# A two-layer decoder trunk: first unit by feature chunk, fused last norm, fp32 router logits, selection by counting, and a first expert turn of its own

## The chip, the cores and the metric

The kernel runs on one core of a Trainium2 chip (trn2). Its time is that of the device, in microseconds, as the median of several runs. TensorE (PE) multiplies, VectorE (DVE), ScalarE (ACT) and GpSimd (POOL) do the elementwise work, and SyncE (SP) issues most transfers. Each engine works through its own queue in order and waits on semaphores.

## The reference

256 tokens of 1024 features pass through two layers, all in float32. Only the parts that the change touches are shown.

```python
for i in range(DEPTH):                                     # DEPTH = 2
    h = rmsnorm(x, g_mix[i])
    u_pool, v_conv, gate_logits = split(h @ w_in[i])       # pooling, conv, gates
    x = x + (gate_pool * y_pool + gate_conv * y_conv) @ w_mix_out[i]
    h = rmsnorm(x, g_xattn[i]); m = rmsnorm(mem, g_mem[i])
    x = x + memory_cross_attention(h, m, w_xq[i], w_xkv[i], w_xo[i])
    h = rmsnorm(x, g_ffn[i])
    if i % 2 == 0: x = x + swiglu(h, w_ffn_gu, w_ffn_down)
    else:          x = x + moe_swiglu(h, w_router, b_router, w_moe_gu, w_moe_down)
return rmsnorm(x, g_final)
# moe_swiglu: logits = h @ w_router + b_router; the two largest of 8 are taken (the lower
# index wins a tie), gates = softmax over the two; each token is the gated sum of its experts
```

## The kernel before

Every large product is computed from two halves of each operand: a high part, rounded to the fast float32 format of TensorE, and the rest. `mm3` issues three products for one: high by high, high by low, low by high. ScalarE makes the high part by a copy (`hi(n)` for weights into `WH`, `norm_hi` for features into `XH`), VectorE the low part by a subtraction (`lo(n)` into `WL`, `norm_lo` into `XL`).

The weights come in units of 128 x 2048 values, 1 MB, in a fixed order (`stream_plan` for the NA units of the two layers, `expert_units` for the 33 of one expert). SP loads them into a ring of 4 slots, and of 11 during the experts; the split halves have 3 slots. Before it loads a slot again SP waits until VectorE has split what was in it. In the program of each engine the order is written out by hand: at unit n, ScalarE and VectorE first split unit n + 2 and then do what belongs to unit n. The banks of PSUM are given out by a plan (`BankPlan`), and `claim` waits for whoever reads a bank's contents of before.

At the start SP issues the two token tiles of x (`xs`), unit 0, the small vectors as rows, and then the other units. ScalarE squares x in four pieces, VectorE makes the variance (L1144), GpSimd the factor (`rstd`, a power, L724), VectorE scales both tiles (L1151), TensorE transposes them into features (16 transposes, L1586) and then the vector rows, VectorE copies the vectors out (L1198 to L1200), and the chunks of features are split (L869 and L1160). Unit 0 multiplies by output tile: all eight chunks for the first 128 columns, then for the second. After unit 1 TensorE transposes the normalised memory (`norm_T("mem", 0)`), which ScalarE has loaded through its own queue and squared, and VectorE has scaled.

After the last unit of layer 1 comes the router. x is transposed, weighted with the gain and split as for any norm; the logits are made feature-major with `mm3` (L1830), copied out and transposed back to tokens (L1841). VectorE scales them, adds the bias, and picks the two largest by maxima and priorities (L1399 to L1413). TensorE ranks the chosen tokens with a triangular product (L1845 to L1850), VectorE builds the one-hot matrix `PMr` from the slots, and TensorE gathers the first expert's rows from the split, normalised x (`gather`, L1861, 32 products of 256 columns). GpSimd computes each token's places in the expert blocks and sends the rows there with indirect transfers. Then the turns: seven to fifteen in a loop (seven here), and a last one written out, each one expert block of 128 rows by 33 units of twelve products. Rows of experts after the first are loaded and transposed during the turn before. In the last turn the results of the earlier turns are added to x in eight pieces (`add_early`, at steps 16 to 23).

At the end VectorE adds the last expert's part, ScalarE squares x in four pieces, VectorE multiplies by the final gain in four pieces (L1546), the factor is made, ScalarE scales tile 0 and VectorE tile 1 (L1123 and L1551), and four stores go out.

## Time and profile before

| | us |
|---|---|
| Median of 3 runs (lowest to highest) | 1464.66 (1464.15 to 1464.69) |
| The profiled execution | 1463.53 |
| Its span, from first to last instruction | 1461.7 |
| TensorE busy in the span | 1420.4 |
| VectorE busy | 1145.3 |
| ScalarE busy | 909.8 |
| Mean granted TensorE clock, share of full | 0.99 |

The profile's times are read from the start of the span. A matmul counts as busy until its modelled end, so back-to-back products overlap, and busy time is no count of work. A row of busy time by window gives the window, its length, then for PE, PEld (TensorE's weight loads), DVE, ACT and POOL the busy us and the number of instructions, then TensorE's granted clock as a share of full (1.00 is 2.4 GHz, 0.50 is 1.2 GHz), the mean busy share of the DMA engines and GB/s. The bracket behind a row of a timeline is the idle time of the engine before it, with the one that ended it.

### The profile page before, as it was taken

The page shows a single profiled execution, that of the slowest core. Times are in us where ns is not written, and L with a number is a line of the kernel's source. Part 1 is how long each engine was busy: PE and PEld are TensorE (multiplying, and loading weights), DVE is VectorE, ACT ScalarE, POOL GpSimd, SP SyncE. Part 2 cuts the span into 40 slices and gives each one's busy share as a digit, 9 for nine tenths or more (in the row PEclk, how much of TensorE's full clock was granted, in tenths as well). Part 3 has the DMA queues.
Part 4 walks back from the last instruction along what each step waited for, and adds up shares of the span by engine and source line. Part 5 has one row for each costly group of instructions (what it writes and reads, how often), then busy time and mean ns, then how long its engine had stood idle before and what let it go on. Part 6 is the DMA issues. An engine that isn't in the chain of part 4 may idle for free.

```text
span 1461.7 us, 20187 instructions
## 1 busy us (share of the span) xinstructions
PE 1420.4 (97%) x7551; PEld 1226.0 (84%) x7551; DVE 1145.3 (78%) x1045; ACT 909.8 (62%) x825; POOL 72.2 (5%) x108
## 2 busy tenths in 40 slices
PE   6999999999999998998999999999999999999997
PEld 6998898888879997886888888888888888888875
DVE  6897855564547997745888888888889889898997
ACT  6444455544344435554677777777777777777774
POOL 1005000000000004000400000000000000000100
PEclk9999999999999999999999999999999999999998
DMA  9565953555554554547899999999999999999990
GB/s 293 171 190 173 340 207 116 185 189 194 181 198 148 190 171 145 173 141 305 306 394 354 400 397 368 392 369 390 395 362 393 378 381 395 361 395 387 379 369 29
DMA packets 189207, 413.13 MB, mean 283 GB/s; under 512 B 8830, under 2 KB 94174, under 8 KB 189150
## 3 DMA queue, kind: packets, MB, share of 16 engines
q1 hardware_dynamic: 184078, 397.62, 75.1%
q0 software_dynamic: 3328, 12.58, 2.3%
q10 hardware_dynamic: 1744, 2.13, 0.4%
q8 instruction: 40, 0.66, 0.2%
q14 instruction: 17, 0.14, 0.0%
HBM read 397.10 MB, written 15.20 MB: 282 GB/s over the span
## 4 chain that ended last, share of the span: by engine, by line
PE 82%; issue 10%; DVE 3%; ACT 2%; POOL 2%; DMA 1%; POOLq 0%; ACTq 0%; SPq 0%; DVEq 0%
PE bank L1569 26%; PE bank L1571 26%; PE bank L1570 26%; PE bank L1897 1%; DVE WL L1138 1%; DVE arena L1183 1%; ACT WH L850 1%; PE bank L1799 0%; PE bank L1818 0%; DMA xrows<-ysb 0%; POOL xn L740 0%; PE bank L1904 0%; PE bank L1602 0%; PE bank L1586 0%; PE bank L1861 0%
## 5 line engine op out<-in xcount | busy, mean ns | idle before, releaser
L1460 DVE TENSOR_TENSOR WL<-arena,WH 128x2048 fp32r<-128x2048 f32 x262 | 596.9, 2291 | 81.2 <-ACT WH L1064 81.2
L1064 ACT ACTIVATE WH<-arena 128x2048 fp32r<-128x2048 f32 x262 | 502.7, 1919 | 127.6 <-PE bank L1571 127.5
L1569 PE MATMUL bank<-WH,XH 128*128 128x512 f32 x1008 | 397.0, 394 | 0.5 <-issue 0.3
L1571 PE MATMUL bank<-WH,XL 128*128 128x512 f32 x1008 | 393.1, 390 | 0.0
L1570 PE MATMUL bank<-WL,XH 128*128 128x512 f32 x1008 | 392.6, 389 | 0.0
L1138 DVE TENSOR_TENSOR WL<-arena,WH 128x2048 fp32r<-128x2048 f32 x109 | 248.5, 2283 | 108.7 <-ACT WH L850 108.7
L850 ACT ACTIVATE WH<-arena 128x2048 fp32r<-128x2048 f32 x109 | 205.9, 1894 | 61.0 <-PE bank L1571 58.9
L1571 PEld LDWEIGHTS bank<-WH,XL 128*128 128x128 f32 x1008 | 189.2, 188 | 39.9
L1569 PEld LDWEIGHTS bank<-WH,XH 128*128 128x128 f32 x1008 | 189.4, 188 | 39.4 <-issue 1.1
L1570 PEld LDWEIGHTS bank<-WL,XH 128*128 128x128 f32 x1008 | 189.5, 188 | 38.0
L1569 PE MATMUL bank<-XH,WH 128*128 128x256 f32 x592 | 169.4, 286 | 5.1 <-DVE XL L1160 3.4
L1570 PE MATMUL bank<-XL,WH 128*128 128x256 f32 x592 | 168.4, 284 | 0.0
L1571 PE MATMUL bank<-XH,WL 128*128 128x256 f32 x592 | 168.3, 284 | 0.0
L1569 PE MATMUL bank<-WH,hThm 128*128 128x512 f32 x352 | 138.9, 395 | 0.4 <-DVE WL L1460 0.4
L1571 PE MATMUL bank<-WH,hTlm 128*128 128x512 f32 x352 | 137.3, 390 | 0.0
L1570 PE MATMUL bank<-WL,hThm 128*128 128x512 f32 x352 | 137.1, 390 | 0.0
L1569 PEld LDWEIGHTS bank<-XH,WH 128*128 128x128 f32 x592 | 114.3, 193 | 6.5 <-issue 3.7
L1570 PEld LDWEIGHTS bank<-XL,WH 128*128 128x128 f32 x592 | 114.5, 193 | 0.1
L1571 PEld LDWEIGHTS bank<-XH,WL 128*128 128x128 f32 x592 | 114.4, 193 | 0.0
L1183 DVE SCALAR_TENSOR_TENSOR arena<-arena,vec 128x256 f32<-128x256 f32 x240 | 97.9, 476 | 0.0
L1569 PEld LDWEIGHTS bank<-WH,hThm 128*128 128x128 f32 x352 | 66.1, 188 | 14.6 <-DVE WL L1460 1.3
L1571 PEld LDWEIGHTS bank<-WH,hTlm 128*128 128x128 f32 x352 | 66.1, 188 | 14.0
(246 smaller groups left out, 1357.3 us busy)
## 6 DMA issues: line engine op xcount, KB each, us to landing
arena<-in_w_moe_gu SPq DMA_DIRECT2D x128, 1024.0 KB, 5.4
arena<-in_w_moe_down SPq DMA_DIRECT2D x88, 1024.0 KB, 7.2
arena<-in_w_moe_gu SPq DMA_DIRECT2D x96, 512.0 KB, 6.1
arena<-in_w_in SPq DMA_DIRECT2D x28, 1024.0 KB, 4.9
arena<-in_w_ffn_gu SPq DMA_DIRECT2D x44, 512.0 KB, 4.6
arena<-in_w_xkv SPq DMA_DIRECT2D x16, 1024.0 KB, 5.3
arena<-in_w_ffn_down SPq DMA_DIRECT2D x11, 1024.0 KB, 4.8
arena<-in_w_mix_out SPq DMA_DIRECT2D x8, 1024.0 KB, 5.0
```

Source lines behind the costliest of these rows:

```text
L850: a.activation(WH[:, n % HL, 0:width(n)], s[:, 0:width(n)], ACT.Copy).then_inc(hi_ready, 1)
L1064: a.activation(WH[:, (NA + i) % HL, :], raw[s], ACT.Copy).then_inc(hi_ready, 1)
L1138: v.tensor_tensor(WL[:, n % HL, 0:w], s[:, 0:w], WH[:, n % HL, 0:w].bitcast(F32), ALU.subtract).then_inc(lo_ready, 1)
L1183: v.scalar_tensor_tensor(acc[:, c, :], cu[:, c, k:k + S], tap(L, k, c), acc[:, c, :], ALU.mult, ALU.add).then_inc(conv_step, 1)
L1460: v.tensor_tensor(WL[:, (NA + i) % HL, :], raw[(i % NM) % RING_M], WH[:, (NA + i) % HL, :].bitcast(F32), ALU.subtract).then_inc(lo_ready, 1)
L1569: te.matmul(out, ah, bh, start=start, stop=False, skip_group_check=shared)
L1570: te.matmul(out, ah, bl, start=False, stop=False, skip_group_check=shared)
L1571: return te.matmul(out, al, bh, start=False, stop=stop, skip_group_check=shared)
L1897: ins = te.transpose(ps[:, c * P:c * P + P], hhm[:, o:o + P], ident[:, :])
```

## The change

It makes five edits.

- **Start.** g_mix is loaded ahead of unit 0, and unit 0 in two halves; unit 1 follows, then the other vectors; the memory's load moves to SP's queue, behind unit 2. VectorE squares tile 1 and scales tile 0, ScalarE squares tile 0 and scales tile 1. TensorE first multiplies an identity 11 and 7 times, transposes g_mix alone, and computes unit 0 by chunk: both output tiles for chunk 0, then for chunk 1, and so on. The other vectors are transposed after unit 0.
- **Logits.** The unscaled x is transposed, copied as fp32 into `xT`, and multiplied in fp32, tokens on the output partitions, by router weights that have taken the gain (`wrg`). Six unused products follow (`WARM`).
- **Selection.** Each logit is compared with each other one; the counts give its rank, the two top ranks are chosen.
- **Gather.** The first expert's rows are gathered in fp32 from x itself; the one-hot matrix carries the norm's factor and the copies out of PSUM the gain. The first turn is written out on TensorE: its gathers 0 to 2 come before unit 0, gather 3 behind it, and each unit waits for its own chunks. The other engines keep their loop.
- **Last norm and early adds.** Only one piece is multiplied by the gain apart; the other three are scaled and weighted in one VectorE instruction each, behind the variance. The early adds stand at steps 13, 14, 17, 18, 21, 22, 25 and 26.

```diff
 HL = 3
+WARM = 6
+EARLY_AT = (13, 14, 17, 18, 21, 22, 25, 26)
+WARM_UP = (11, 7)
...
-            sp.dma_start(wdst("a", 0), wsrc(*units[0])).then_inc(raw_landed[0], 16)
-            r = 0
-            for src in (g_mix, g_xattn, g_mem, g_ffn, pool_scale, b_dw, conv_ln_g, conv_ln_b):
+            sp.dma_start(rows[0:DEPTH * KC, 0, :], g_mix.rearrange("l (k p) -> (l k) p", p=P)).then_inc(gmix_in, 16)
+            sp.dma_start(wdst("a", 0)[:, 0:4], wsrc(*units[0])[:, 0:4]).then_inc(first_half, 16)
+            sp.dma_start(wdst("a", 0)[:, 4:8], wsrc(*units[0])[:, 4:8]).then_inc(raw_landed[0], 16)
+            sp.dma_start(wdst("b", 1), wsrc(*units[1])).then_inc(raw_landed[1], 16)
+            r = DEPTH * KC
+            for src in (g_xattn, g_mem, g_ffn, pool_scale, b_dw, conv_ln_g, conv_ln_b):
...
-            for n, (kind, L, j) in list(enumerate(units))[1:]:
+            for n, (kind, L, j) in list(enumerate(units))[2:]:
+                if n == 3:
+                    sp.dma_start(mem_in, mem[0].rearrange("(t p) d -> p t d", p=P)).then_inc(mem_in_s, 16)
...
-            squares(norm_id("mix", 0), xs, BY_TILE, lambda i, t: (x_in[t], 16))
-            hi(0)
-            act.dma_start(mem_in, mem[0].rearrange("(t p) d -> p t d", p=P)).then_inc(mem_in_s, 16)
+            act.wait_ge(c_one, 1)
+            a.activation(unused[:, 0:1], ones[:, 0:1], ACT.Square)
+            act.wait_ge(x_in[0], 16)
+            a.activation(xn[:, 0, :], xs[:, 0, :], ACT.Square, scale=D ** -0.5,
+                         accum_out=ss[:, 0, 0, 0:1]).then_inc(sq_done, 2)
+            act.wait_ge(first_half, 16)
+            a.activation(WH[:, 0, 0:1024], raw[0][:, 0:1024], ACT.Copy).then_inc(hi_half, 1)
+            act.wait_ge(rstd_ready, 1)
+            a.activation(xn[:, 1, :], xs[:, 1, :], ACT.Copy, scale=rs[:, 0, 1:2]).then_inc(x1_scaled, 1)
...
+            for b in range(4):
+                act.wait_ge(*full(("norm", 0, b)))
+                if b == 0:
+                    a.activation(XH[:, 0, :], bk(("norm", 0, 0))[:, 0:S], ACT.Copy,
+                                 scale=gcol("mix", 0, 0)).then_inc(first_hi, 1)
...
+                if b == 1:
+                    act.wait_ge(raw_landed[0], 16)
+                    a.activation(WH[:, 0, 1024:2048], raw[0][:, 1024:2048], ACT.Copy).then_inc(hi_ready, 1)
...
+                if (kind, L, j) == ("xo", 1, 2):
+                    x_squares("ffn", L, "xo", 0)
+                    for i in range(2):
+                        act.wait_ge(*full(("xT", i)))
+                        a.activation(xT[:, 2 * i:2 * i + 2, :], bk(("xT", i))[:, :].rearrange("p (c s) -> p c s", c=2),
+                                     ACT.Copy).then_inc(xT_early, 1)
...
+                    act.wait_ge(x_gained, 4)
+                    for t in range(NT):
+                        a.activation(xn[:, t, :], xn[:, t, :], ACT.Copy, scale=rs[:, N, t:t + 1]).then_inc(xn_ready, 1)
...
-                    a.activation(XH[:, 2 * b:2 * b + 2, 0:P], gathered(b), ACT.Copy).then_inc(g_hi, 1)
+                    for c in range(2):
+                        ins = a.activation(XH[:, 2 * b + c, 0:P], gathered(b)[:, c, :], ACT.Copy,
+                                           scale=gcol("ffn", 1, 2 * b + c))
+                    ins.then_inc(g_hi, 1)
...
-            norm_scale(norm_id("mix", 0), xs)
-            lo(0)
+            dve.wait_ge(x_in[1], 16)
+            v.scalar_tensor_tensor(xn[:, 1, :], xs[:, 1, :], 1.0 / D, xs[:, 1, :], ALU.mult, ALU.mult,
+                                   accum_out=ss[:, 0, 1, 0:1]).then_inc(sq_done, 2)
+            dve.wait_ge(sq_done, 4)
+            v.tensor_scalar(vv[:, 0, :], ss[:, 0, :, 0], EPS, None, ALU.add).then_inc(var_ready, 1)
...
+            v.tensor_scalar(xn[:, 0], xs[:, 0], rs[:, 0, 0:1], None, ALU.mult).then_inc(xn_ready, 2)
+            dve.wait_ge(hi_half, 1)
+            v.tensor_tensor(WL[:, 0, 0:1024], raw[0][:, 0:1024], WH[:, 0, 0:1024].bitcast(F32),
+                            ALU.subtract).then_inc(lo_half, 1)
...
+                if b == 1:
+                    dve.wait_ge(hi_ready, 1)
+                    v.tensor_tensor(WL[:, 0, 1024:2048], raw[0][:, 1024:2048], WH[:, 0, 1024:2048].bitcast(F32),
+                                    ALU.subtract).then_inc(lo_ready, 1)
...
+                def x_with_gain(m):
+                    for t in range(NT):
+                        dve.wait_ge(sq_done, 4 * norm_id("ffn", 1) + 2 * m + t + 1)
+                        ms = slice(m * 512, m * 512 + 512)
+                        v.tensor_tensor(xn[:, t, ms], xs[:, t, ms], gain_rows[:, ms], ALU.mult).then_inc(x_gained, 1)
...
+                    def xT_copy(i, t, c0, nc_):
+                        dve.wait_ge(*full(("xT", i)))
+                        v.tensor_copy(xT[:, c0:c0 + nc_, t * P:t * P + P],
+                                      bk(("xT", i))[:, 0:nc_ * P].rearrange("p (c s) -> p c s", c=nc_)
+                                      ).then_inc(xT_late, 1)
+                    xT_copy(2, 0, 4, 4)
+                    xT_copy(3, 1, 4, 2)
+                    norm_var(norm_id("ffn", L))
+                    xT_copy(4, 1, 6, 2)
+                    x_with_gain(1)
...
+            link(v.tensor_tensor(beats[:, :, :, :], LOG.unsqueeze(3).to_broadcast([P, NT, NE, NE]),
+                                 LOG.unsqueeze(2).to_broadcast([P, NT, NE, NE]), ALU.is_ge))
+            link(v.tensor_tensor(beats[:, :, :, :], beats[:, :, :, :],
+                                 tri[:, :, :].unsqueeze(1).to_broadcast([P, NT, NE, NE]), ALU.mult))
+            v.tensor_reduce(BEATEN, beats[:, :, :, :].rearrange("p t a b -> p t b a"), X_AXIS, ALU.add
+                            ).then_inc(route, 1)
+            rt[0] += 1
+            link(v.tensor_reduce(BEATS, beats[:, :, :, :], X_AXIS, ALU.add))
+            link(v.tensor_tensor(RANK, BEATEN, BEATS, ALU.subtract))
+            ranks = top[:, :].unsqueeze(1).to_broadcast([P, NT, NE])
+            v.tensor_tensor(SEL, RANK, ranks, ALU.is_lt).then_inc(sel_ready, 1)
...
+                v.tensor_scalar(PM[:, t, :], iota[:, :], slotT[:, t, 0:1], rs[:, norm_id("ffn", 1), t:t + 1],
+                                ALU.is_equal, ALU.mult).then_inc(PM0_ready, 1)
...
+            gather_lo((0, 1), lambda b: b + 1)
+            lo(NA + 1)
+            gather_lo((2, 3), lambda b: b + 1)
...
-                    if last and 16 <= i < 24:
-                        add_early(i - 16)
+                    if last and i in EARLY_AT:
+                        add_early(EARLY_AT.index(i))
...
+            v.tensor_tensor(xv, xv, fin_gain[:, 0:4, :], ALU.mult).then_inc(gained, 1)
+            norm_var(N)
+            dve.wait_ge(rstd_ready, N + 1)
+            for r in range(1, 4):
...
+                v.scalar_tensor_tensor(xn[:, t, ms].rearrange("p (c s) -> p c s", c=4),
+                                       xs[:, t, ms].rearrange("p (c s) -> p c s", c=4), rs[:, N, t:t + 1],
+                                       fin_gain[:, 4 * m:4 * m + 4, :], ALU.mult, ALU.mult).then_inc(out_ready, 1)
...
+            for i in range(WARM_UP[0]):
+                te.matmul(bank[2][:, 0:P], ident[:, :], ident[:, :], start=True, stop=True)
+            pe.wait_ge(gmix_in, 16)
...
+            done(te.transpose(ps[:, 0:R0], rows[0:R0, 0, :], ident[0:R0, 0:R0]), ("vec",))
+            for i in range(WARM_UP[1]):
+                te.matmul(bank[2][:, 0:P], ident[:, :], ident[:, :], start=True, stop=True)
+            for kk in range(2):
...
+            to_feature_major("mix", 0, xn, lambda t: (x1_scaled, 1) if t else (xn_ready, 1), (1, 2, 3))
+            def other_vectors():
+                pe.wait_ge(gmix_in, 16)
+                pe.wait_ge(rows_in, 16 * (7 + 1 + 1))
+                ps = claim(("vec2",))
+                te.transpose(ps[:, 0:VROWS], rows[0:VROWS, 0, :], ident[0:VROWS, 0:VROWS])
+                R = TAPS * CC
+                for L in range(DEPTH):
+                    te.transpose(ps[:, P + L * R:P + L * R + R], rows[0:R, 1 + L, :], ident[0:R, 0:R])
+                done(te.matmul(ps[:, 504:504 + NE], ones[0:1, :], brow[0:1, :], start=True, stop=True), ("vec2",))
...
+                for k in range(KC):
+                    if k % 4 == 0:
+                        pe.wait_ge(*((lo_ready, 1) if k else (lo_half, 1)))
+                    pe.wait_ge(ht_lo if k else first_lo, k // 2 + 1)
+                    for ct in range(2):
+                        cs = slice(ct * P, ct * P + P)
+                        ins = mm3(ps[:, ct * S:ct * S + S], wh[:, k, cs], wl[:, k, cs], XH[:, k, :], XL[:, k, :],
+                                  (k, ct) == (0, 0), (k, ct) == (KC - 1, 1), True)
...
+                for kk in chunks:
+                    ins = te.matmul(bk(("logits",))[:, t * NE:t * NE + NE], xT[:, kk, t * P:t * P + P], wrg[:, kk, :],
+                                    start=(t, kk) == (0, 0), stop=(t, kk) == (1, KC - 1), skip_group_check=True)
...
+            pe.wait_ge(x_add, xadd(1, "xo", 2))
+            late_xT(2, 0, range(4, KC))
+            pe.wait_ge(wrg_ready, 1)
+            pe.wait_ge(xT_early, 2)
+            claim(("logits",))
+            logits(0, (0, 1))
+            pe.wait_ge(x_add, xadd(1, "xo", 3))
+            late_xT(3, 1, (4, 5))
+            late_xT(4, 1, (6, 7))
+            logits(0, (2, 3))
+            logits(1, range(4))
+            pe.wait_ge(xT_late, 1)
+            logits(0, range(4, KC))
+            pe.wait_ge(xT_late, 2)
+            logits(1, (4, 5))
+            pe.wait_ge(xT_late, 3)
+            done(logits(1, (6, 7)), ("logits",))
+            for i in range(WARM):
+                te.matmul(bank[4][:, :], XH[:, 0, 0:P], XH[:, 0:2, :].rearrange("p c s -> p (c s)"), start=True,
+                          stop=True)
+            pe.wait_ge(sel_ready, 3)
...
+                ps = claim(("gather", b))
+                for t in range(NT):
+                    pe.wait_ge(PM0_ready, t + 1)
+                    for c in range(2):
+                        kk = 2 * b + c
+                        ins = te.matmul(ps[:, c * 2 * P:c * 2 * P + P], xs[:, t, kk * P:kk * P + P], PM[:, t, :],
+                                        start=(t, c) == (0, 0), stop=(t, c) == (NT - 1, 1), skip_group_check=True)
+                done(ins, ("gather", b))
+            for b in range(3):
+                gather(b)
...
-                    if i == 0:
+                    if first and i == 1:
+                        gather(3)
+                    if first and i < 4:
+                        pe.wait_ge(g_lo, i + 1)
+                    if first and i == 4:
+                        for bb in (0, 5, 2, 3):
+                            pe.wait_ge(*read(plan.last[bb]))
...
-            with pe.Fori(0, n) as it:
+            turn_tensor(0, False, True)
+            with pe.Fori(1, n) as it:
                 turn_tensor(it, False)
```

## Rows read from the trace of the kernel before

**Rows 1.** The page of the profile, its first line and part 1

```profile
span 1461.7 us, 20187 instructions
...
PE 1420.4 (97%) x7551; PEld 1226.0 (84%) x7551; DVE 1145.3 (78%) x1045; ACT 909.8 (62%) x825; POOL 72.2 (5%) x108
```

**Rows 2.** Busy time by window, expert turns (columns: see the profile section)

```profile
795.00:888.00 93.00, 93.00 (x426) 77.21 (x425) 82.54 (x48) 70.87 (x51) 0.00 (x0) 1.00 1.02 389
...
sum 744.00, PE 743.22 PEld 615.52 DVE 662.23 ACT 564.04 POOL 19.15; mean PE 92.90 PEld 76.94 DVE 82.78 ACT 70.51 POOL 2.39
```

**Rows 3.** Who TensorE waited for: us in total, times, longest

```profile
PE bank L1586 <- DVE xn L1151: 9.1, 1, 9.1
...
PE bank L1845 <- DVE lg L1413: 3.6, 1, 3.6
...
PE bank L1569 <- DVE WL L1460: 0.6, 2, 0.4
```

**Rows 4.** Timeline of the first 20 us: start, us, engine, line, operation

```profile
4.47 0.63 ACT L857 ACTIVATE xn<-xs 128x512 f32<-128x512 f32 x1 [2.38 <-DMA xs<-in_x]
...
8.19 1.42 DVE L1151 TENSOR_SCALAR xn<-xs,rs 128x1024 f32<-128x1024 f32 x2 [0.92 <-POOL rs L724]
8.75 1.91 ACT L850 ACTIVATE WH<-arena 128x2048 fp32r<-128x2048 f32 x1 [1.66 <-DMA arena<-in_w_in]
...
9.09 4.03 PE L1586 MATMUL bank<-ident,xn 128*128 128x128 f32 x16 [9.09 <-DVE xn L1151]
...
15.27 2.65 ACT L869 ACTIVATE XH<-bank,vec 128x256 fp32r<-128x256 f32 x7
15.89 3.23 DVE L1160 SCALAR_TENSOR_TENSOR XL<-bank,vec,XH 128x256 fp32r<-128x256 f32 x8 [1.03 <-ACT XH L869]
...
16.91 0.36 PE L1569 MATMUL bank<-XH,WH 128*128 128x256 f32 x1 [2.75 <-DVE XL L1160]
```

**Rows 5.** Timeline of TensorE, the memory's transposes

```profile
29.98 1.91 PE L1586 MATMUL bank<-ident,xn 128*128 128x128 f32 x16
```

**Rows 6.** Busy time by window at the start

```profile
0.00:20.00 20.00, 8.03 (x37) 7.39 (x38) 8.56 (x17) 10.65 (x20) 4.17 (x21) 0.93 0.95 310
18.00:19.00 1.00, 1.00 (x6) 1.00 (x6) 1.00 (x3) 1.00 (x1) 0.00 (x0) 0.50 1.10 345
```

**Rows 7.** Timeline from the last sum of x to the rank product

```profile
682.26 0.69 DVE L1192 TENSOR_TENSOR xs<-xs,bank 128x512 f32<-128x512 f32 x1 [2.03 <-PE bank L1571]
...
689.30 0.35 DVE L1387 SCALAR_TENSOR_TENSOR lg<-bank,rs,bias 128x8 f32<-128x8 f32 x2
...
692.16 0.59 PE L1845 MATMUL bank<-lg,upper 128*128 128x8 f32 x2 [3.56 <-DVE lg L1413]
...
693.03 0.57 PE L1847 MATMUL bank<-lg,upper 128*128 128x8 f32 x2
```

**Rows 8.** Busy time by window around the router

```profile
690.00:692.00 2.00, 0.00 (x0) 0.00 (x0) 1.76 (x12) 2.00 (x2) 0.00 (x0) 0.50 0.80 317
...
698.00:700.00 2.00, 2.00 (x11) 2.00 (x11) 1.97 (x2) 0.52 (x2) 1.89 (x2) 0.50 0.00 0
```

**Rows 9.** Timeline of the first expert units

```profile
702.14 0.49 PE L1569 MATMUL bank<-WH,XH 128*128 128x512 f32 x1 [0.26 <-issue]
...
703.19 3.91 ACT L1064 ACTIVATE WH<-arena 128x2048 fp32r<-128x2048 f32 x2
...
705.14 4.49 DVE L1460 TENSOR_TENSOR WL<-arena,WH 128x2048 fp32r<-128x2048 f32 x2 [1.91 <-ACT WH L1064]
```

**Rows 10.** Timeline of the last norm and the stores

```profile
1454.13 0.19 ACT L857 ACTIVATION_READ_ACCUMULATOR xn<-xs 128x1 f32 x1
1455.28 0.15 DVE L1144 SCALAR_TENSOR_TENSOR vv<-ss 128x2 f32<-128x2 f32 x1
...
1455.51 1.11 POOL L724 TENSOR_TENSOR rs<-vv,mhalf 128x2 f32<-128x2 f32 x1 [78.91 <-DVE vv L1144]
...
1458.58 0.35 ACTq L1126 DMA_DIRECT2D out<-xn  x1
```

322 lines of the change are left out of this document (155 added, 167 removed).

## The prediction

> **What bounds the kernel now.** I read the page first, then who waited for whom on TensorE, then the busy time by stage, and last the timeline of the three stretches where TensorE stands still. The page shows a program that is TensorE's nearly everywhere: busy 97% of 1461.7 us [rows 1]. An expert turn of 93 us has it busy for all 93.00 us at full clock, with VectorE at 82.5 and ScalarE at 70.9, and over all eight turns it is busy 743.2 of 744 us [rows 2]. The diff leaves the arithmetic of a turn alone, so the turns can't become shorter. What is left is TensorE's idle time, and the waits say where it is [rows 3]: 9.1 us before the first transpose, 3.6 us in front of the router's rank product, and only 0.6 us inside the expert turns. The change works on three places: the start, the router up to the third expert unit, and the last norm. I cost each by the time at which TensorE (or the last store) leaves that place, since all that comes behind moves along with it.
>
> **Start, before.** x is squared from 4.47, both tiles are scaled by 9.6, 16 transposes take 4.03 us, then the gain vectors, then eight feature chunks on ScalarE (2.65 us for seven, 0.38 each) and VectorE (3.23 us for eight, 0.40 each); the first product issues at 16.91 [rows 4]. The first two units end where the memory transposes begin, 29.98 [rows 5]. The granted clock around 18 was 0.50, the lower level of 1.2 GHz, after 2.75 us without work [rows 4, 6]. Those 96 products in 13.1 us come out at 0.12 each at full clock, if the lower one lasted some 3.5 us.
>
> **Start, after, step by step.** Between 4.47 (tile 0 there) and 8.75 (unit 0 there) tile 1 and the two halves of unit 0 land, 1.43 us per half megabyte: tile 1 at 5.9, the first half at 7.3 [rows 4]. VectorE squares tile 1 in about 1.2 us (half of its 2.3 us subtraction, taken from the pair of 4.49 [rows 9]): 7.1. The way from variance to factor took 1.1 us before (7.1 to 8.19): 8.2, no gain yet. VectorE scales tile 0 (0.71) to 8.9. ScalarE splits half a unit (half of 1.91) from 7.3 and scales tile 1 in 1.0: 9.3. The first chunk's transposes run at once, its high half is copied by 10.1, its low half stands at 10.6; the pitch is 0.40 from there. The second half of unit 0's weights costs ScalarE 0.96 and VectorE 1.15 after chunk 3, so chunk 7 is complete at 15.3. Then unit 1: ScalarE (1.91) to 16.0, VectorE (2.3) to 18.3. TensorE does six products per chunk, 0.72 us at full clock, from 11.3 to 17.3, and the vector transposes that were moved behind them to 18.0. Unit 1 starts at 18.3, bound by its weights; 48 products of 0.12 are 5.75 us: end at 24.0. Saving against 29.98: **6.0 us**. If the whole first unit ran at 1.2 GHz it would end up to 1.5 us behind unit 1's weights: 4.5. The 18 warm-up products cost nothing, as TensorE has nothing else to do up to 9.3; without that cover each would cost 0.2 to 0.4.
>
> Moved along: the memory's load leaves ScalarE's queue and stands in SP's behind units 1 and 2 and the small vector loads. 310 GB/s over the first 20 us are 6.2 MB [rows 6]; x, three units, the vectors and the memory are 5.6, so it lands near 18.5. Squares (four pieces, 2.6 us), variance and power (1.1) and scaling (1.4) end near 23.6, and TensorE asks at 24.0. That cover is thin; behind it each us later costs one us, since unit 2 is queued behind these transposes.
>
> **Router, before.** The last sum of x ends at 682.95, logits start on VectorE at 689.30, TensorE gets the selection at 692.16 and does a small fp32 product in 0.43 us (two in 0.87) [rows 7]. The clock is 0.50 at 690 to 692 and still at 698 to 700 [rows 8]. The first expert product comes at 702.14; ScalarE starts on expert units 2 and 3 at 703.19 and VectorE at 705.14, so unit 2 is ready at 707.4 [rows 9]. Units 0 and 1 hold TensorE for 2 x 2.73 us (33 units of twelve products and some transposes fill a turn, at most 2.8 each [rows 2]), to 707.6: no stall.
>
> **Router, after.** x is transposed as it is, and 16 fp32 products with eight columns (32 instructions) replace the 24 split ones. No row has one at full clock. Bounds: 0.43 as read, and half of it, 0.22. With 0.22, eight transposes of 0.12 (1.91 for 16 [rows 5]) and 0.4 of wait for the late sum, logits are complete at 687.1. Selection on VectorE: two logit rows (0.35), then four operations over 128 elements, for which the nearest rows are 0.18 (eight elements [rows 7]) and 0.40 (256 elements [rows 4]); I take 0.29, then two short ones of 0.2: 1.9 us, selection at 689.0. Rank product and five short steps to 690.0, slots and first one-hot tile 690.4. The gather turns into fp32 with 128 columns, one product for two of 256: again 0.22 to 0.43. Three of four pieces, 12 products, take 2.7: 693.1. So expert unit 0 starts at 693.4, almost 9 us earlier. But that isn't kept. The fourth piece (0.9) now comes behind unit 0 (2.73): 697.1. ScalarE is a queue in order, and unit 2's split stands behind that copy: before, 1.3 us lay between the last gather product (702.14 less the issue gap of 0.26) and the split at 703.19; the copy in two parts adds 0.2. So the split runs from 698.6 to 700.5, VectorE to 702.8. TensorE is done with unit 1 at 699.9 and waits some 3 us; unit 2 starts at 702.9 to 703.5, against 707.6. I take **4.2 us**. Data isn't late: DMA stood still at 698 to 700 [rows 8], with the ring of eleven units full. The gained x (VectorE, four of 0.69) and its scaling (ScalarE, two of 1.0) end near 688, hidden: GpSimd wants them only after the slots. GpSimd's own steps, done by 702 before, feed a load of turn 0's later half.
>
> **Last norm.** The last read-out ends at 1454.32, but the variance starts at 1455.28, because three gain products stand ahead of it on VectorE; the power takes 1.11 us and the last store is issued at 1458.58 [rows 10]. After: variance at 1454.35, power between 0.72 (as at the start) and 1.11, then three fused products of 0.68 instead of two scalings of ScalarE in a row: the last store is ready at 1457.3 to 1457.7. Saving **1.0 us**. Spreading the early adds can recover at most the 0.6 us of waits inside the turns; I count nothing.
>
> **Sum.** 6.0 + 4.2 + 1.0 = 11.2 us. The profiled execution took 1463.53 us (its span and 1.8 around it) and would take 1452.3; the median of the runs is 1.1 above it, so I forecast 1453.5.
>
> **The clock, and what the skill says.** TensorE was at 1.2 GHz through both the router's small products and most of the gather, after 3.6 us without work [rows 7, 8]. The change fills part of that hole with useful products and six idle ones, and leaves less than 1 us in one piece. The Trainium skill, TensorE: Matmul & The Clock Gate (Part 1: The HAM clock gate), holds that the throttled state is the default, that only sustained activity lifts it, and that the switching point differs from run to run. If loads with eight columns aren't activity, the clock falls under the new router as under the old, which is rival (a); by that rule the saving would be 8.1 us or less, not 11.2. No row here settles it.
>
> **Rivals.** (a) *The router runs at 1.2 GHz.* For it: it did before. Against: the hole is shorter. Rank product and 12 gather products then cost 3.1 us more (0.2 each): 1456.6; with the logits slow too, 16 times 0.21, another 3 us: 1459.5. (b) *The start gives half.* Unit 0's first half or the memory lands 3 us late: 1456.5. For it: the DMA share is 0.95 over the first 20 us [rows 6], so nothing there has slack. Against: the byte count above. (c) *Slower than before.* TensorE's program now has the turn three times in its code. Were its instructions fetched too slowly, the pitch of the products in the turns would grow: 744 us of turns times 1.5% is 11.2 us, the point where it eats the gain; at 2.5% the time is 1472. Against: the loop of before fetches as many instructions in each turn and has no gap [rows 2].
>
> **Chances and range.** Forecast 0.52, (a) 0.28, (b) 0.14, (c) 0.03, and 0.03 for a hidden loss that cancels the gain. A measurement of this kernel can tell 0.2%, 2.9 us, from no change. So: faster 0.93 or a little more, within 0.04, slower 0.03. The range goes from the best prices (6.5, 4.8 and 1.2 us saved with a run at the low end, and the early adds' 0.6) to (a) nearly whole: 1451.3 to 1459.0.
>
> **What would show it.** The first product near 11 us and the memory transposes near 24; the selection at 689; the first expert product near 693, then a wait of TensorE of about 3 us for the weights of unit 2; the variance right behind the last square. I am wrong if the clock column has 0.5 from 688 on, if TensorE waits over 1 us for the memory rows, or if a turn takes more than 93.2 us.

## The result, and the profile after

The changed kernel takes 1456.36 us in the median of five runs (1453.81 to 1457.07), against 1464.15 (1461.93 to 1464.69, five runs) of the kernel before: ratio 0.9944, interval 0.9933 to 0.9955. By the medians that is 7.8 us less, by the ratio 8.2. I had forecast 1453.5. The profiled execution took 1454.71 us with a span of 1453.0, against a span of 1461.7 before [rows 1], so it gained 8.7 us.

The page's first line and part 1, and who TensorE waited for (us in total, times, longest):

```profile
span 1453.0 us, 20257 instructions
...
PE 1424.2 (98%) x7600; PEld 1230.7 (85%) x7600; DVE 1142.0 (79%) x1043; ACT 907.8 (62%) x817; POOL 70.8 (5%) x110
```

```profile
PE bank L1643 <- DVE WL L1535: 3.0, 1, 3.0
...
PE bank L1696 <- ACT xn L920: 1.2, 1, 1.2
...
PE bank L1660 <- DVE xn L1199: 1.1, 2, 0.8
```

The waits of 9.1 us ahead of the first transpose and of 3.6 ahead of the rank product [rows 3] are gone from the table. The first is only filled, though: the first transpose of x starts at 9.09 in both kernels, behind warm-up products now. New are 3.0 us for the weights of expert unit 2, 1.2 for tile 1 of x, and 1.1 for the memory rows.

**Start.** The timelines of ScalarE and TensorE, first 29 us:

```profile
8.46 1.06 ACT L918 ACTIVATE WH<-arena 128x1024 fp32r<-128x1024 f32 x1 [2.78 <-DMA arena<-in_w_in]
...
18.90 1.91 ACT L875 ACTIVATE WH<-arena 128x2048 fp32r<-128x2048 f32 x1 [2.10 <-DMA arena<-in_w_in]
21.74 0.63 ACT L882 ACTIVATE xn<-arena 128x512 f32<-128x512 f32 x1 [0.92 <-DMA arena<-in_mem]
```

```profile
10.99 1.47 PE L1660 MATMUL bank<-ident,xn 128*128 128x128 f32 x12
12.25 0.36 PE L1643 MATMUL bank<-XH,WH 128*128 128x256 f32 x1
...
26.20 0.30 PE L1660 MATMUL bank<-ident,xn 128*128 128x128 f32 x1 [0.79 <-DVE xn L1199]
26.77 1.86 PE L1660 MATMUL bank<-ident,xn 128*128 128x128 f32 x15 [0.27 <-DVE xn L1199]
28.39 0.36 PE L1643 MATMUL bank<-XH,WH 128*128 128x256 f32 x1
```

The first half of unit 0 is there at 8.46, where I had 7.3; the memory at 21.7, where I had 18.5. Unit 2's first product, behind the memory's transposes, comes at 28.39. Before, those transposes began at 29.98 [rows 5], and the product followed at 31.64: 3.3 us saved. The line of before, and DMA up to the memory's landing in the changed kernel:

```profile
31.64 0.36 PE L1569 MATMUL bank<-XH,WH 128*128 128x256 f32 x1
```

```profile
0.00:21.70 21.70, 18.04 (x125) 17.05 (x126) 11.76 (x18) 12.41 (x17) 4.55 (x23) 1.00 0.95 299
```

**Router.** VectorE's last sum of x and its split of unit 2, ScalarE's copies of gather pieces 2 and 3 and its splits, TensorE at unit 2:

```profile
678.90 0.69 DVE L1240 TENSOR_TENSOR xs<-xs,bank 128x512 f32<-128x512 f32 x1 [2.04 <-PE bank L1645]
...
697.63 4.49 DVE L1535 TENSOR_TENSOR WL<-arena,WH 128x2048 fp32r<-128x2048 f32 x2 [1.96 <-ACT WH L1113]
```

```profile
690.73 0.62 ACT L1095 ACTIVATE XH<-bank,vec 128x128 fp32r<-128x128 f32 x2 [0.27 <-PE bank L1996]
694.40 0.63 ACT L1095 ACTIVATE XH<-bank,vec 128x128 fp32r<-128x128 f32 x2 [3.05 <-PE bank L1996]
...
695.68 5.51 ACT L1113 ACTIVATE WH<-arena 128x2048 fp32r<-128x2048 f32 x3
```

```profile
700.07 0.76 PE L1643 MATMUL bank<-WH,XH 128*128 128x512 f32 x1 [2.97 <-DVE WL L1535]
```

ScalarE does nothing for 3.05 us between the third and the fourth copy, and its split of unit 2 stands behind both. Units 0 and 1 last only to 696.9. Busy time by window, with the granted clock in the third column from the right:

```profile
682.00:684.00 2.00, 2.00 (x13) 1.95 (x14) 0.40 (x3) 1.91 (x3) 0.00 (x0) 0.72 1.04 412
684.00:686.00 2.00, 2.00 (x6) 1.48 (x5) 1.80 (x9) 0.42 (x1) 0.00 (x0) 0.50 1.02 406
...
698.00:700.00 2.00, 0.00 (x0) 0.00 (x0) 2.00 (x2) 2.00 (x2) 1.75 (x1) 0.98 1.01 414
700.00:702.00 2.00, 1.93 (x5) 1.58 (x6) 2.00 (x1) 1.19 (x1) 1.92 (x2) 0.50 1.13 342
```

The clock is at 1.2 GHz twice. By windows of 1 us it falls at about 682.9, in the last of the logits (679.1 to 683.5), and stays down through the six idle products to 686.3; TensorE counts as busy all that time. It falls again at 699.9, as the wait for unit 2 ends. The long low stretch of before [rows 8] has become two.

The router ends, for this comparison, with TensorE's first hidden transposes of turn 0, in the kernel before and in the changed one:

```profile
726.78 1.04 PE L1897 MATMUL bank<-ident,sh 128*128 128x128 f32 x8
```

```profile
720.75 1.03 PE L2026 MATMUL bank<-ident,sh 128*128 128x128 f32 x8
```

Counted from the start of the last sum of x (682.26 [rows 7] and 678.90) that is 44.5 us before and 41.9 after: 2.7 us saved.

**Last turn and last norm.** The first three sets of hidden transposes of the last turn, and VectorE at the end:

```profile
1373.41 1.03 PE L2026 MATMUL bank<-ident,sh 128*128 128x128 f32 x8
...
1407.12 1.04 PE L2026 MATMUL bank<-ident,sh 128*128 128x128 f32 x8
...
1429.86 0.60 PE L2026 MATMUL bank<-ident,sh 128*128 128x128 f32 x4
```

```profile
1446.65 0.16 DVE L1192 SCALAR_TENSOR_TENSOR vv<-ss 128x2 f32<-128x2 f32 x1 [0.19 <-ACT xn L882]
1447.65 2.08 DVE L1623 SCALAR_TENSOR_TENSOR xn<-xs,rs,fin_gain 128x512 f32<-128x512 f32 x3 [0.84 <-POOL rs L749]
```

The transposes are 33.71 and 22.74 us apart. The kernel before had them at 1379.46, 1413.36 and 1437.57:

```profile
1413.36 1.04 PE L1897 MATMUL bank<-ident,sh 128*128 128x128 f32 x8
...
1437.57 0.60 PE L1897 MATMUL bank<-ident,sh 128*128 128x128 f32 x4
```

That is 33.90 and 24.21, so 1.66 us are gained inside the last turn. From the last square's sum to the end of the span it was 7.6 us (1454.13 [rows 10] to 1461.7) and is 6.6 (1446.43 to 1453.0): 1.0 us. The four parts, 3.3 + 2.7 + 1.7 + 1.0, are the 8.7 us of the spans in their tenths.

### The profile page after: what moved, and what is told of

It reads as the page before. It is cut to its first block, busy times and chain, and to the rows that moved or that the text cites. A ratio compares the mean times of both kernels' runs of the same rounds, so it can differ in the third digit from the quotient of the medians.

```text
span 1453.0 us, 20257 instructions
## 1 busy us (share of the span) xinstructions
PE 1424.2 (98%) x7600; PEld 1230.7 (85%) x7600; DVE 1142.0 (79%) x1043; ACT 907.8 (62%) x817; POOL 70.8 (5%) x110
## 4 chain that ended last, share of the span: by engine, by line
PE 86%; issue 6%; DVE 2%; ACT 2%; POOL 2%; DMA 1%; SPq 1%; ACTq 0%; POOLq 0%; DVEq 0%
PE bank L1643 27%; PE bank L1645 27%; PE bank L1644 27%; PE bank L2026 1%; PE bank L1920 1%; PE bank L1939 1%; DVE WL L1186 1%; DMA arena<-in_mem 1%; DVE arena L1231 1%; DMA xrows<-ysb 1%; POOL xn L765 0%; PE bank L2033 0%; ACT WH L875 0%; SPq L609 0%; PE bank L1676 0%
## 5 line engine op out<-in xcount | busy, mean ns | idle before, releaser
L1535 DVE TENSOR_TENSOR WL<-arena,WH 128x2048 fp32r<-128x2048 f32 x262 | 596.6, 2291 | 81.5 <-ACT WH L1113 81.4
L1113 ACT ACTIVATE WH<-arena 128x2048 fp32r<-128x2048 f32 x262 | 502.6, 1919 | 128.4 <-PE bank L1645 128.4
L1186 DVE TENSOR_TENSOR WL<-arena,WH 128x2048 fp32r<-128x2048 f32 (+1 forms) x108 | 246.3, 2284 | 108.0 <-ACT WH L875 108.0
L875 ACT ACTIVATE WH<-arena 128x2048 fp32r<-128x2048 f32 (+1 forms) x108 | 203.9, 1894 | 60.4 <-PE bank L1645 57.6
```

The costliest lines, as they stand in the source:

```text
L875: a.activation(WH[:, n % HL, 0:width(n)], s[:, 0:width(n)], ACT.Copy).then_inc(hi_ready, 1)
L1113: a.activation(WH[:, (NA + i) % HL, :], raw[s], ACT.Copy).then_inc(hi_ready, 1)
L1186: v.tensor_tensor(WL[:, n % HL, 0:w], s[:, 0:w], WH[:, n % HL, 0:w].bitcast(F32), ALU.subtract).then_inc(lo_ready, 1)
L1535: v.tensor_tensor(WL[:, (NA + i) % HL, :], raw[(i % NM) % RING_M], WH[:, (NA + i) % HL, :].bitcast(F32), ALU.subtract).then_inc(lo_ready, 1)
```

## The experiments

Each ratio is to the kernel before, run on the same chip. Times of that kernel there were 1463.5 to 1464.4 us in the median.

**e1: the early adds back where they were.**

```diff
-EARLY_AT = (13, 14, 17, 18, 21, 22, 25, 26)
+EARLY_AT = tuple(range(16, 24))
```

> The changed kernel with the eight early adds of the last turn back in steps 16 to 23, one per step. Theory (the adds overloaded VectorE): the last turn lost about 1.6 us in the kernel before, hidden in waits too short for the wait table, so this run is 1.6 us slower than the changed kernel, with the last turn's hidden transposes 33.9, 24.2 us apart again. Rival (the wait table is complete): at most 0.6 us slower, and the 1.65 us come from elsewhere, from the data or the DMA of that execution.

**e2: the kernel before, with the early adds spread.**

```diff
-                    if last and 16 <= i < 24:
-                        add_early(i - 16)
+                    if last and i in (13, 14, 17, 18, 21, 22, 25, 26):
+                        add_early((13, 14, 17, 18, 21, 22, 25, 26).index(i))
```

> The kernel before with only the places of the eight early adds changed to 13, 14, 17, 18, 21, 22, 25 and 26. Theory: 1.6 us faster than the kernel before (ratio 0.9989), all of it between the second and third set of hidden transposes of the last turn. Rival: 0.6 us or less, ratio 0.9996 or nearer to one.

e1 took 1458.46 us (0.9957, interval 0.9943 to 0.9971), 2.1 above the changed kernel. e2 took 1461.92 (0.9985, 0.9976 to 0.9994), 2.2 us under the kernel before. TensorE's timeline of e1, then of e2:

```profile
1409.61 1.04 PE L2026 MATMUL bank<-ident,sh 128*128 128x128 f32 x8
...
1433.93 0.60 PE L2026 MATMUL bank<-ident,sh 128*128 128x128 f32 x4
```

```profile
1414.20 1.04 PE L1897 MATMUL bank<-ident,sh 128*128 128x128 f32 x8
...
1436.94 0.60 PE L1897 MATMUL bank<-ident,sh 128*128 128x128 f32 x4
```

24.2 to 24.3 us with the adds in a row, 22.74 with them spread, in either kernel. The theory that the adds in a row cost some 1.6 us holds. VectorE's groups of the kernel before, 1402 to 1427 (busy us, mean ns, then idle before), show how:

```profile
L1460 DVE TENSOR_TENSOR WL<-arena,WH 128x2048 fp32r<-128x2048 f32 x9 | 20.6, 2284 | 0.0
L1490 DVE SCALAR_TENSOR_TENSOR xs<-early,early_gate,xs 128x512 f32<-128x512 f32 x4 | 3.0, 745 | 0.0
```

VectorE has no idle time there, and a split with an add (2.20 + 0.66) is issued every 2.87 us, while TensorE needs 2.73 for a unit. The waits are not all too short for the wait table, as my expectation had it: it lists two, of 0.2 and 0.4 us. But it counts only from a product's modelled end (0.39), which overhangs the next start (0.23) by 0.16. By the starts, the products at 1420.08 and 1429.27 come 0.36 and 0.56 us late, the one behind each takes 0.11 more, and one at 1410.51 comes 0.20 late and is not in the table. All starts more than 0.29 us apart, from the first hidden transposes of the last turn to the third, add up to 1.8 us beyond the 0.23 before and to 0.3 in the changed kernel.

**e3: all four gather pieces ahead of expert unit 0.**

```diff
-            for b in range(3):
+            for b in range(4):
                 gather(b)
...
-                    if first and i == 1:
-                        gather(3)
```

> The changed kernel with all four gather pieces in front of expert unit 0. Theory (ScalarE's queue: the split of unit 2 stands behind the copy of the fourth piece, and TensorE's clock falls only because of the 3.0 us wait): expert unit 0 starts about 0.9 us later, the copy of piece 3 ends about 2.7 us earlier, TensorE waits less than 0.5 us for unit 2, the granted clock stays at 1.00 from 686 on, and the kernel is 2.5 to 3.5 us faster than the changed one, near 1453. Rival 1 (the clock would fall anyway, as it follows the small router products): only the wait shrinks, 1.5 to 2 us. Rival 2 (VectorE's split of unit 2 is bound by VectorE's own queue): no gain, TensorE waits as before at unit 2.

1451.59 us (0.9912, 0.9899 to 0.9926), 4.8 under the changed kernel in the median, more than the 2.5 to 3.5 I had expected. Between the two profiles the router is 2.6 us shorter. ScalarE and TensorE:

```profile
694.49 0.63 ACT L1095 ACTIVATE XH<-bank,vec 128x128 fp32r<-128x128 f32 x2 [0.27 <-PE bank L1996]
...
695.79 3.72 ACT L1113 ACTIVATE WH<-arena 128x2048 fp32r<-128x2048 f32 x2
```

```profile
700.18 0.47 PE L1643 MATMUL bank<-WH,XH 128*128 128x512 f32 x1 [0.26 <-DVE WL L1535]
```

The wait is 0.26 us, and no low stretch follows it. Here the clock was low from 685.6 to 692.5, from the idle products through rank products and gather, so the part of the theory that the clock stays up from 686 on is wrong: the first low stretch is not caused by the wait, only the second is.

**e4: the memory's load on ScalarE's queue.**

```diff
-                if n == 3:
-                    sp.dma_start(mem_in, mem[0].rearrange("(t p) d -> p t d", p=P)).then_inc(mem_in_s, 16)
...
             a.activation(xn[:, 1, :], xs[:, 1, :], ACT.Copy, scale=rs[:, 0, 1:2]).then_inc(x1_scaled, 1)
+            act.dma_start(mem_in, mem[0].rearrange("(t p) d -> p t d", p=P)).then_inc(mem_in_s, 16)
```

> The changed kernel with the memory's load issued from ScalarE's queue, behind the scaling of tile 1 (about 10.5 us), and taken out of SP's queue in front of unit 3. Theory (the memory was late because it stood behind the others in SP's queue): it lands 1 to 3 us earlier than 21.7, ScalarE does its squares right behind the split of unit 2, the waits of 1.1 us at the memory's transposes go, and unit 1's end to the end of the memory transposes takes 2.0 instead of 3.2 us: 1 us faster than the changed kernel. Rival (DMA bandwidth is the limit: 310 GB/s): the memory lands earlier only as unit 2 or the vectors land later, so the gain is under 0.3 us or it is slower.

1459.28 us (0.9965, 0.9953 to 0.9977): 2.9 us above the changed kernel where I had expected 1 below. My theory fell. ScalarE and TensorE:

```profile
20.45 1.91 ACT L873 ACTIVATE WH<-arena 128x2048 fp32r<-128x2048 f32 x1 [3.64 <-DMA arena<-in_w_in]
```

```profile
27.01 0.30 PE L1659 MATMUL bank<-ident,xn 128*128 128x128 f32 x1 [1.60 <-DVE xn L1198]
27.58 3.45 PE L1659 MATMUL bank<-ident,xn 128*128 128x128 f32 x15 [0.27 <-DVE xn L1198]
```

The load was issued at 8.46 and no longer held up the squares, but unit 2 landed at 20.45 instead of 18.90, which fits the rival: one bandwidth is shared. The squares stand behind unit 2's split, so the wait at the memory's transposes grew from 0.79 to 1.60 us. The clock fell half a us behind it, stayed at 1.2 GHz for about 3.4 us, and fifteen transposes took 3.45 us for 1.86.

**e5: the kernel before, with the new start alone** (all edits of the start in the diff above, nothing else).

> The kernel before with the start of the changed one alone (first unit by chunks, warm-up products, the halves of unit 0, the memory's load in SP's queue); router, last norm and early adds as before. Theory (the traces show the start's whole gain and it is kept to the end): the memory transposes end 3.3 us earlier and the kernel is 3.3 us faster, ratio 0.9977. Rival 1 (my forecast for the start): 6.0 us, ratio 0.9959. Rival 2 (the gain is given back later): under 1 us.

1459.32 us (0.9972, 0.9961 to 0.9983): 4.1 us saved, interval 2.5 to 5.7. The 3.3 lies in it, the 6.0 does not, and nothing is given back. This execution alone saved 4.7 us (31.64 less 26.93, and as much in the span), so what the start is worth differs with the execution. In it unit 2 landed at 17.48, the memory's squares began at 20.28, TensorE did not wait, and unit 2's first product came at 26.93. In the profiles of the kernels that keep this start and its load order, that product came at 26.93 (e5), 27.08 (e7), 27.17 (e1), 27.87 (e8), 28.07 (e12), 28.29 (e3) and 28.39 (the changed kernel); in the three with the old start at 30.64 (e2), 31.64 and 31.79 (e11). The later ones are those in which unit 2 and the memory landed later.

**e6: e3, with the memory ahead of unit 2** on SP's queue, on ScalarE and on VectorE.

```diff
+            sp.dma_start(mem_in, mem[0].rearrange("(t p) d -> p t d", p=P)).then_inc(mem_in_s, 16)
             for n, (kind, L, j) in list(enumerate(units))[2:]:
-                if n == 3:
...
+                if (kind, L, j) == ("a", 0, 0):
+                    squares(norm_id("mem", 0), mem_in, BY_TILE, lambda i, t: (mem_in_s, 16))
                 if n < NA - 1 and (kind, j) != ("cout", 1):
                     hi(n + 2)
...
```

> The changed kernel with four gather pieces in front of expert unit 0 and, at the start, the memory's load put in front of unit 2's on SP's queue, its squares in front of the split of unit 2 on ScalarE, and its scaling in front of unit 2's low half on VectorE. Theory (all loads of the start share one bandwidth, so it is their order that counts): the memory lands near 19 and unit 2 near 21.7; the wait of 1.1 us at the memory's transposes goes and unit 2 is still in time (needed at 27.0): 1.0 to 1.3 us faster than with the four pieces alone, near 1450.5. Rival (unit 2 is now late, as it was with the memory on ScalarE's queue): TensorE waits after the memory's transposes instead, and the time is 1 to 3 us longer than 1451.6.

1450.83 us (0.9912, 0.9899 to 0.9926): by the times not to be told from e3. ScalarE's timeline shows the rest:

```profile
17.30 0.63 ACT L881 ACTIVATE xn<-arena 128x512 f32<-128x512 f32 x1 [0.62 <-DMA arena<-in_mem]
...
21.09 1.92 ACT L874 ACTIVATE WH<-arena 128x2048 fp32r<-128x2048 f32 x1 [1.22 <-DMA arena<-in_w_in]
```

TensorE has no wait at the memory's transposes any more, and unit 2's first product comes at 26.77, 27.02 and 26.87 in the three profiles with this order (e6, e9, e10). It takes the spread of 1.5 us out of the start, at its early end. In the profile of e6 the router gave the gain back: its low stretch lasted 10.2 us, against 6.8 in e3.

**e7: e3 without the six idle products (WARM = 0).**

> The changed kernel with four gather pieces in front of expert unit 0 and without the six idle products in front of the router's rank product. Theory (the clock falls because the products with eight columns and the wait for the selection keep TensorE too idle; it falls within the logits, ahead of the six products): the low stretch starts at most 1 us earlier and ends no later, and the time is within 1 us of 1451.6. Rival (the six products shorten the low stretch): the low stretch lasts 3 to 4 us longer, as with the kernel before (10 us), and the time is 1.5 us or more above 1451.6.

1452.58 us (0.9925, 0.9911 to 0.9938). The low stretch runs from 683.6 to 690.4, as long as in e3. The six products don't change it; TensorE waits 2.2 us for the selection in their place. The time is 1.0 us above e3, at the edge of the 1 us that the theory named. Its place for the fall was wrong in both: the logits end at about 684.4 in e3 and 682.7 in e7, and the clock falls at 685.6 during the idle products, and at 683.6 in the wait.

**e8: the changed kernel without the 18 warm-up products (WARM_UP = (0, 0)).**

> The changed kernel without the 18 warm-up products at the start. Theory (TensorE has idled in front of the first chunk, and the clock is then low through much of the first unit, as it was low at 17.4 to 20.8 in the kernel before): a stretch of 3.4 us or more at 1.2 GHz within 12 to 20 us; the first unit is bound by its products there, and the memory's transposes come 0 to 1.5 us later than 25.4, so the kernel is up to 1.5 us slower than the changed one. Rival (the start is bound by loads, not by TensorE): no difference, as the wait for the memory's rows takes it up.

1457.02 us (0.9955, 0.9942 to 0.9969), not to be told from the changed kernel. TensorE's transposes of x and its first product, and a window behind them:

```profile
10.84 2.68 PE L1660 MATMUL bank<-ident,xn 128*128 128x128 f32 x12
13.26 0.38 PE L1643 MATMUL bank<-XH,WH 128*128 128x256 f32 x1
```

```profile
12.00:16.00 4.00, 4.00 (x31) 4.00 (x30) 3.24 (x7) 4.00 (x8) 0.00 (x0) 1.00 1.11 301
```

No low stretch lies in the first unit, whose products follow each other every 0.12 us. So my theory fell in the place it named. But the warm-up does something: without it the twelve transposes take 2.68 us instead of 1.47, 421 ns each as in the kernel before instead of 272, though the clock column reads 1.00 there in all three. The first product comes 1.0 us later than in the changed kernel, although the first half of unit 0 landed 0.5 us earlier (8.00). The changed kernel's lead is lost at the memory, which lands at 21.7 there and at 21.2 here: unit 2's first product comes at 28.39 and at 27.87. The rival's end came true, and the two profiles fit its reason.

**e9: e6 with wider logits products**, and **e12: the changed kernel with them alone.** Only the first 8 of the 64 columns are read.

```diff
...
-                    ins = te.matmul(bk(("logits",))[:, t * NE:t * NE + NE], xT[:, kk, t * P:t * P + P], wrg[:, kk, :],
+                    ins = te.matmul(bk(("logits",))[:, t * 64:t * 64 + 64].rearrange("p (r e) -> p r e", e=NE),
+                                    xT[:, kk, t * P:t * P + P], wrg[:, kk, :].unsqueeze(1).to_broadcast([P, 8, NE]),
```

> The memory-first kernel (e6) with one edit: each of the 16 fp32 logits products of the router takes its eight columns of weights eight times over, so it writes 64 columns where it wrote 8; the first eight of them are read, the rest is unused. At full clock a product should cost no more than half of a gather product of 128 columns, 0.11 us, about what it costs now. Theory (the fall of the granted clock at 681 is brought on by the router's small products): the clock stays at 1.00 through the logits or falls only behind them, and the time is 1 to 3 us under e6's 1450.8. Rival (the fall comes from something else): the clock falls at 681 as in e6, the wider products cost up to 0.11 us more each there, and the time is 0 to 2 us above e6.

> The changed kernel as it is, with the wider logits products of e9 alone. Theory: the first of its two low stretches (3.4 to 7 us from 683 on) goes or shrinks, the second, behind the 3 us wait for unit 2, stays: 0 to 2 us faster than the changed kernel's 1456.4, as the time up to the wait is partly bound by ScalarE and VectorE. Rival: both low stretches stay, and the time is the same or up to 2 us longer.

e9 took 1450.08 us (0.9911, 0.9898 to 0.9925), e12 1456.78 (0.9956, 0.9942 to 0.9969). Windows of e6, then of e9:

```profile
680.00:682.00 2.00, 2.00 (x15) 2.00 (x15) 0.31 (x1) 1.91 (x3) 0.00 (x0) 0.73 1.05 416
...
688.00:690.00 2.00, 2.00 (x11) 2.00 (x11) 0.77 (x3) 0.62 (x2) 1.45 (x8) 0.50 0.00 0
```

```profile
680.00:682.00 2.00, 2.00 (x18) 1.96 (x18) 0.66 (x2) 1.90 (x3) 0.00 (x0) 1.00 1.03 406
...
688.00:690.00 2.00, 2.00 (x17) 1.86 (x16) 1.72 (x4) 1.47 (x6) 1.74 (x4) 1.00 0.00 0
```

TensorE counts as equally busy in both; with eight columns the clock fell (at 680.9, the logits ending at 681.8), with 64 it stayed full through logits, rank products and gather. At full clock the first two logits products, four instructions, took 0.51 us with 8 columns and 0.56 with 64, so the width costs next to nothing. The router is 3.9 us shorter in e9's profile than in e6's, but by the times the two are not to be told apart (0.9911 and 0.9912), so the 1 to 3 us that I had expected are not shown. In e12 the first low stretch is gone and the second, behind the 3 us wait (2.97), stays from 699.7 to 703.1. Its time is no better, and its router only 0.45 us shorter: unit 2 is ready at 699.24, for ScalarE's queue sets that.

**e10: e9 with nine idle products for six.**

> The same kernel as e9 with nine idle products in place of six behind the logits. In e6 TensorE came out of the six just as the selection was ready, at 1.2 GHz; at 2.4 GHz six take half of that and leave about 1 us without work. Theory: nine fill it (2.1 us at full clock against 2.3 us from logits to selection) and the clock stays up for rank products and gather: 0 to 2 us faster than e9. Rival: the fall is not put off by them, or they run at the lower level and delay the rank products by up to 1.5 us: slower than e9.

1448.86 us (0.9901, 0.9885 to 0.9916), the fastest kernel of the study, 15 us under the kernel before. From e9 its times don't tell it, and its router takes as long. So the nine do nothing that the six don't.

**e11: the kernel before, with the new last norm alone.**

> The kernel before with the last norm of the changed one alone. Theory: the variance starts right behind the last square, the power takes 0.72 in place of 1.11 us, and the kernel is 1.0 us faster, ratio 0.9993, which its times can hardly tell from no change; the profile shows 8.7 us from the last square's end to the end of the span in place of 9.7. Rival (the stores are the limit): the last store is issued 1 us earlier and the span's end does not move with it.

1462.65 us (0.9991, 0.9982 to 1.0), by the times alone hardly to be told from no change. From the last square's sum (1454.29) to the end of the span (1460.9) it is 6.6 us, against 7.6 in the kernel before. The 8.7 and 9.7 of my expectation were wrong as lengths; their difference, 1.0 us, is what the profile shows. VectorE:

```profile
1454.51 0.16 DVE L1144 SCALAR_TENSOR_TENSOR vv<-ss 128x2 f32<-128x2 f32 x1 [0.19 <-ACT xn L858]
1455.51 2.08 DVE L1548 SCALAR_TENSOR_TENSOR xn<-xs,rs,fin_gain 128x512 f32<-128x512 f32 x3 [0.84 <-POOL rs L725]
```

**The router in all profiles.** From the start of the last sum of x to TensorE's first hidden transposes of turn 0, read from the timelines; what lies between those transposes and the same ones of the last turn is 652.7 to 652.8 us in every kernel.

| kernel | us | low clock within it | wait for unit 2 |
|---|---|---|---|
| before; e11; e5; e2 | 44.52; 44.58; 44.49; 44.97 | one stretch, about 10 us | none |
| changed; e8 | 41.85; 41.87 | two, about 3.4 us each | 2.97; 2.96 |
| e4; e1 | 44.79; 45.25 | two, about 6.8 us each | 3.37; 3.51 |
| e12 | 41.40 | the second alone, about 3.4 us | 2.97 |
| e3; e7; e6 | 39.26; 39.09; 40.86 | the first alone, about 7; 7; 10 us | 0.26; 0.22; 0.74 |
| e9; e10 | 36.98; 37.02 | none | 0.22; 0.21 |

## Why the forecast was right, and where it was not

The direction, the three places and the price of the last norm were right; the range held. The time was 2.9 us above the forecast, and that is a sum of misses of both signs. That it stayed within the range is in part luck: start and router lost 4.2 us against the forecast, and the early adds, which I had put at nothing, gave 1.7 back. The median, 1456.36, also lies on the figures of rivals (a) and (b), 1456.6 and 1456.5, with neither of them true as I had put it.

Two of my own three signs of being wrong came up. The clock column has 0.50 behind the point that was 688 before (684.6 here), and TensorE waited 1.1 us for the memory rows. The turns did not grow.

**Start: 6.0 forecast, 3.3 in the profile.** The step that failed is the landing times. Tile 1 came at 5.9 as forecast, but "the first half at 7.3" became 8.46, which put the first product at 12.25 instead of 11.3. The memory was to land "near 18.5", worked out as bytes over bandwidth; it landed near 21.7. The bandwidth was nearly right, 299 GB/s up to 21.7, but that is 6.5 MB, where I had counted the 5.6 up to and with the memory. SP issues unit 3 at 13.18, while the memory is under way, so my estimate is that 0.9 MB of later loads had moved by then. The small vectors stand ahead of the memory too: SP spends 3.26 us on the issue of g_xattn alone, unit 2 is issued at 10.34 and the memory at 10.78. Of the 2.7 us lost, 1.0 lies ahead of the first product, 0.3 between it and the end of unit 1, and 1.5 at the memory's transposes, which TensorE begins 0.95 us behind that end and which take 2.19 us instead of 1.66. So rival (b), "the memory lands 3 us late", had the landing right, but it cost 1.5 us and not 3, as TensorE was late itself. e4 and e6 show that the remedy is the order of the loads and not the queue, since a load that comes sooner makes another later. The step "if the whole first unit ran at 1.2 GHz" did not occur, with or without warm-up products (e8); what ran at half pace without them were the transposes.

**Router: 4.2 forecast, 2.7 in the profile, nothing in other executions.** The steps up to the wait were right: the selection, forecast for 689 on the time scale of the kernel before, was ready on VectorE at 685.8, which is 689.2 there (the last sum of x is 3.36 us earlier), and TensorE took it up at 686.2; unit 2 started at 700.07, which is 703.4, forecast for 702.9 to 703.5; the fourth copy held up ScalarE's split of unit 2, and TensorE waited 3.0 us for it. e3 shows it as the cause: with the fourth piece in front, the wait and the low stretch behind it are gone, and the kernel is faster. The step that failed is that I priced this wait at its 3 us alone and left out what it does to the clock: 3.4 us at half clock cost up to 1.7 us, which is most of the 1.5 missing. The clock fell during this wait or within 0.5 us behind its end in all five profiles that have it (the changed kernel, e1, e4, e8, e12). The trace of before had such waits too. In the layers TensorE waits 2.9 us near 150 and 3.4 near 577, and the clock is low behind both:

```profile
150.34 0.47 PE L1569 MATMUL bank<-SH,WH 128*128 128x256 f32 x1 [2.88 <-DVE WL L1138]
```

```profile
150.00:152.00 2.00, 1.66 (x8) 1.66 (x9) 2.00 (x2) 1.56 (x1) 0.00 (x0) 0.62 0.99 360
```

Every kernel here has these two waits, and a low stretch lies at 27 of the 28, not at the first one of e7. Rival (a) expected the low level in rank products and gather, at 1456.6. It was there in e3, but in the changed kernel's profile the low stretches lay in the end of the logits with the idle products, and in unit 2.

The stretches vary. Where each was about 3.4 us long, the router took 41.9 us, where each was about 6.8 us, 44.8 to 45.3, as much as before the change. So the change in the router is worth 2.7 us or nothing, as the stretches fall. The five runs of the changed kernel fit this: 1453.81 and 1454.71 have a mean granted clock of 0.993, 1456.36 to 1457.07 have 0.991 and 0.992. My profile is of the first kind, and the median 1.65 us above it, not 1.1. That the slower three had the longer stretches is inferred from their mean clock; they have no profile. Nor is it shown that these lay in the router: the low stretches in the layers vary as well, about 3.4 us in most profiles, 6.8 in one place of e2, e3 and e7. From unit 2's first product at the start to the last sum of x it is 650.3 to 650.7 us in eleven profiles, and 651.2, 651.8 and 652.2 in e7, e3 and e2.

The Trainium skill, TensorE: Matmul & The Clock Gate (Part 1: The HAM clock gate), has the clock set by how busy the array has been of late. This case's traces agree for the wait, and narrow it for the logits: by the profile TensorE was busy 2.00 of 2.00 us in the windows in which the clock fell (682 to 684 here, 680 to 682 in e6). So busy time in the profile does not tell whether the clock holds. Where it fell was not always in the logits: so it was in the changed kernel, e6 and e8, but in e1, e3 and e4 it fell 0.6 to 1.3 us behind them, during the wide idle products, and in e7, without these, 0.9 us behind them in the wait. That the logits bring it on rests on the three profiles with wider ones, in which the stretch is gone.

**Early adds: nothing forecast, 1.66 measured.** The step was "spreading the early adds can recover at most the 0.6 us of waits inside the turns". The wait table counts each wait from a modelled end, and leaves out what is shorter than the overhang and the slow product behind a wait. The rate was in the rows: VectorE without idle time at 2.87 us per unit against TensorE's 2.73.

**Last norm: 1.0 forecast, 1.0 measured,** with the power at 0.72 us beside no VectorE work, for 1.11 before [rows 10].

**Sum.** 11.2 became 8.7: start 2.7 less, router 1.5 less, early adds 1.7 more. **Slower by instruction supply** did not occur: from the first hidden transposes of turn 0 to those of the last turn it is 652.7 us in both kernels.

## What to carry to other kernels

Cost a new wait of some 3 us on TensorE twice, once for itself and once for the products behind it at half clock, and move work in front of it where that is possible (e3: a fourth gather piece of some 0.8 us ahead, for 2.6 us in the profiles and 4.8 in the medians). Where a chain of tiny products feeds a decision, look at the granted clock, not at busy time: the same number of instructions with more columns took 0.56 us for four instead of 0.51 and kept the clock up, though the times do not show a gain. To see whether an in-order engine lags, compare periods between two landmarks of the loop, since a wait table counts too little of each stall, by the modelled overhang.

## What the runs showed of the hardware that I had not expected

- 32 instructions of fp32 products of 128 x 8, in a stretch in which the profile has TensorE busy 100%: the granted clock fell to 0.50 during them or within 1.3 us behind them in all seven profiles that have them; with 128 x 64 it stayed at 1.00 there in all three (e9, e10, e12).
- Of 33 waits of TensorE of 2.88 to 3.51 us in these profiles (two in the layers of each kernel, five in front of expert unit 2), 32 had the clock fall to 0.50 for 3.4 or 6.8 us, at a point between 1.1 us before and 1.6 us behind the end of the wait. In front of unit 2, waits of 0.74 us and less had no such stretch.
- One wait of 1.6 us (e4), with sixteen transposes behind it, had such a stretch: 3.45 us for fifteen of them, against 1.86.
- Without products ahead of them, the first transposes of x took 421 ns each (before, e8), with 18 warm-up products ahead 272, while the granted clock read 1.00 in both cases.
- The issue of one 8 KB load took SP 3.26 us when it stood behind x and units 0 and 1 (3.29 in e4, 2.8 to 3.2 in e6 and e8), against 0.42 for the ones behind it.
